# One transfer of 1 MB in place of two of 512 KB for each unit of weights

## What is computed

```python
for layer in range(2):
    h = h + hybrid_mixer(rms_norm(h, norm_mix_g[layer]), ...)   # w_in 1024x2560, w_out 1024x1024
    hn = rms_norm(h, norm_ffn_g[layer])
    if layer == 0: h = h + swiglu(hn, ffn_w1, ffn_w3, ffn_w2)      # 1024x3072, 1024x3072, 3072x1024
    else:          h = h + moe_swiglu(hn, router_w, expert_w1, expert_w3, expert_w2)
return rms_norm(h, final_g)                                     # 8 experts, top 2, hidden width 3584

def swiglu(x, w1, w3, w2):
    return (silu(x @ w1) * (x @ w3)) @ w2
```

## Time and profile before

| | us |
|---|---|
| median of 3 runs | 2086.88 |
| the profiled execution | 2092.64 |
| its span, first to last instruction | 2090.7 |
| TensorE matmuls busy | 2011.1 |
| VectorE busy | 1544.3 |
| ScalarE busy | 1207.3 |

### The profile page before, as it was taken

How to read it: one execution, slowest core, us unless ns; L and a number is a source line. 1 busy time by engine, 2 the same in 40 slices (tenths; PEclk the granted TensorE clock), 3 DMA queues, 4 the chain that set the end, 5 groups by cost and what they waited for, 6 DMA issues and landing times.

```text
span 2090.7 us, 33644 instructions
## 1 busy us (share of the span) xinstructions
PE 2011.1 (96%) x11091; PEld 1743.4 (83%) x11092; DVE 1544.3 (74%) x1694; ACT 1207.3 (58%) x1557; POOL 89.8 (4%) x132
## 2 busy tenths in 40 slices
PE   8999999999999998999999999999999999999992
PEld 7777888888897778999999888888998888888991
DVE  6896666666678976766766698898666888987655
ACT  4533555545554434554655577787555777875543
POOL 1000000000000003000000000000000000000002
PEclk9999999999999999999999999999999999999996
DMA  7321666666543214777777699999776999997743
GB/s 217 122 71 54 222 217 209 216 192 190 184 150 126 87 61 139 269 231 236 252 247 244 225 377 365 368 387 344 251 244 214 365 368 367 387 350 262 247 147 135
DMA packets 245442, 488.18 MB, mean 233 GB/s; under 512 B 16724, under 2 KB 86468, under 8 KB 245396
## 3 DMA queue, kind: packets, MB, share of 16 engines
q1 hardware_dynamic: 237668, 462.04, 64.8%
q0 software_dynamic: 7728, 25.52, 3.5%
HBM read 473.20 MB, written 14.30 MB: 233 GB/s over the span
## 4 chain that ended last, share of the span: by engine, by line
PE 78%; DVE 10%; issue 5%; ACT 3%; DMA 3%; POOL 1%; DVEq 0%; POOLq 0%; ACTq 0%; SPq 0%
PE PS L1430 76%; DVE wlo L724 2%; ACT whi L355 2%; DVE PS L865 2%; DMA raw<-in_expert_w 1%; DVE OV L839 1%; DVE OV L853 1%; DVE OV L1000 1%; PE PS L1758 1%; PE PS L1460 0%; DVE OV L869 0%; DMA OV<-in_norm_mix_g 0%; DVE OV L835 0%; DMA OV<-y_rows,addr 0%; PE PS L1682 0%
## 5 line engine op out<-in xcount | busy, mean ns | idle before, releaser
L724 DVE TENSOR_TENSOR wlo<-raw,whi 128x1024 fp32r<-128x1024 f32 x882 | 1044.0, 1221 | 154.8 <-ACT whi L355 149.1
L355 ACT ACTIVATE whi<-raw 128x1024 fp32r<-128x1024 f32 x882 | 896.7, 1053 | 156.1 <-DMA raw<-in_expert_w 76.6
L1430 PE MATMUL PS<-XN,whi 128*128 128x512 f32 (+3 forms) x3328 | 956.0, 363 | 15.0 <-DVE OV L1000 9.3
L1430 PE MATMUL PS<-XN,wlo 128*128 128x152 f32 (+3 forms) x2944 | 775.1, 263 | 0.0
L1430 PEld LDWEIGHTS PS<-XN,whi 128*128 128x128 f32 x3328 | 617.9, 189 | 84.1 <-DVE OV L1000 15.2
L1430 PE MATMUL PS<-whi,XN 128*128 128x512 f32 x2272 | 671.3, 394 | 8.8 <-DVE XN L874 3.5
L1430 PEld LDWEIGHTS PS<-XN,wlo 128*128 128x128 f32 x2944 | 561.1, 191 | 13.0
L1430 PEld LDWEIGHTS PS<-whi,XN 128*128 128x128 f32 x2272 | 423.6, 188 | 103.7 <-issue 6.9
L1430 PE MATMUL PS<-wlo,XN 128*128 128x512 f32 x1248 | 424.5, 391 | 0.0
L1430 PEld LDWEIGHTS PS<-wlo,XN 128*128 128x128 f32 x1248 | 234.4, 188 | 50.6
L567 ACT ACTIVATE OV<-PS 128x352 f32<-128x352 f32 x112 | 51.6, 461 | 139.9 <-PE PS L1430 139.9
(11 more groups left out here) (214 smaller groups left out, 967.0 us busy)
## 6 DMA issues: line engine op xcount, KB each, us to landing
raw<-in_expert_w SPq DMA_DIRECT2D x672, 512.0 KB, 5.1
raw<-in_ffn_w SPq DMA_DIRECT2D x144, 512.0 KB, 3.7
raw<-in_w_in SPq DMA_DIRECT2D x40, 512.0 KB, 5.4
raw<-in_w_out SPq DMA_DIRECT2D x16, 512.0 KB, 4.6
y_rows<-OV POOLq DMA_DIRECT2D x14, 512.0 KB, 4.4
y_rows<-OV POOLq DMA_DIRECT2D x14, 192.0 KB, 4.9
RES<-in_x SPq DMA_DIRECT2D x4, 512.0 KB, 5.8
x_tok<-OV POOLq DMA_DIRECT2D x4, 512.0 KB, 2.9
```

The source lines that it names most:

```text
L355: act.activation(whi[:, u0 % CONV, half(h)], raw[:, r, half(h)], ACT.Copy).then_inc(s["hi_done"], 1)
L724: dve.tensor_tensor(wlo[:, w, half(h)], raw[:, u0 % RAW, half(h)], whi[:, w, half(h)].bitcast(F32), ALU.subtract).then_inc(s["lo_done"], 1)
L1430: return pe.matmul(out_, lhsT, rhs, start=start, stop=stop, skip_group_check=True)
```

## The change

Each unit is brought by one transfer of 1 MB, which waits until both halves of the slot are done, and signals once. The six semaphores of `raw` become three. The splits stay in halves; the wait of both halves is now for the same semaphore.

```diff
@@ names
-... x3 raw00 raw01 raw10 raw11 raw20 raw21 prm_in ...
+... x3 raw0 raw1 raw2 prm_in ...
@@ load (SyncE)
-                for h in range(2):
-                    if not (isinstance(du, int) and u0 + du < RAW):
-                        sp.wait_ge(s["lo_done"], du * 2 + (2 * (u0 - RAW) + h + 1))
-                    sp.dma_start(raw[:, u0 % RAW, half(h)].rearrange("p (a b) -> p a b", a=parts // 2),
-                                 src[:, h * parts // 2:(h + 1) * parts // 2, :]).then_inc(s[f"raw{u0 % RAW}{h}"], 16)
+                if not (isinstance(du, int) and u0 + du < RAW):
+                    sp.wait_ge(s["lo_done"], du * 2 + (2 * (u0 - RAW) + 2))
+                sp.dma_start(raw[:, u0 % RAW, :].rearrange("p (a b) -> p a b", a=parts),
+                             src).then_inc(s[f"raw{u0 % RAW}"], 16)
@@ the 5 empty units at the end (SyncE)
-                for h in range(2):
-                    sp.wait_ge(s["lo_done"], n_more * (2 * UNITS) + (2 * (u - RAW) + h + 1))
-                    sp.sem_inc(s[f"raw{u % RAW}{h}"], 16)
+                sp.wait_ge(s["lo_done"], n_more * (2 * UNITS) + (2 * (u - RAW) + 2))
+                sp.sem_inc(s[f"raw{u % RAW}"], 16)
@@ split (ScalarE)
                 for h in halves:
-                    act.wait_ge(s[f"raw{r}{h}"], q * 16 + 16 * (u0 // RAW + 1))
+                    act.wait_ge(s[f"raw{r}"], q * 16 + 16 * (u0 // RAW + 1))
                     act.activation(whi[:, u0 % CONV, half(h)], raw[:, r, half(h)],
                                    ACT.Copy).then_inc(s["hi_done"], 1)
```

More of the change, by code:

```diff
@@ L154, in build_program @@
         l_rows = nc.dram_tensor("l_rows", [WIN * VIS, 1], U32)
-        names = """near_sel near_pos last_wout last_add last_ss last_xt last_T last_hi last_lo small_ok x0 x1 x2 x3 raw00 raw01 raw10 raw11 raw20 raw21 prm_in bd_in gB0_in gB_in gF_in rw_in
+        names = """near_sel near_pos last_wout last_add last_ss last_xt last_T last_hi last_lo small_ok x0 x1 x2 x3 raw0 raw1 raw2 prm_in bd_in gB0_in gB_in gF_in rw_in
           const_ok bd_zero step prm_T prm_ok lam_exp sp_ok rw_hi rw_ok warm_up
```

## The result

The changed kernel takes 2129.82 us (median of 4 runs, 2125.66 to 2132.54) and the kernel before 2088.03 (4 runs, 2086.76 to 2090.77). The ratio is 1.0195, with a 95% interval of 1.0175 to 1.0215. So the change costs 2.0%, some 42 us, where +6.8 us was predicted; the time lies above the stated range, which ended at 2117. The profiled execution took 2127.4 us, its span is 2125.7. (The profiled execution after the change is near the low end of its four runs; the one of before, 2092.64, lies above all four of its runs. So the two spans differ by less than the medians.)

The account below looks back on a forecast made before the run. TensorE was taken to bound the kernel, with transfers just keeping up in light visits. Terms 3.0 + 0.8 + 1.9 + 1.1 = +6.8 us took the profiled 2092.64 to 2099.4; predicted median 2093.7, range 2086 to 2117.

Parts of the forecast that it names:

- The landing: Time from issue of a 1 MB weight transfer until it has arrived in its slot, taken as 4.95 us.
- The hold: A ring slot is held from issue to the end of VectorE's second half: 0.1 + 4.95 + 3.45 = 8.50 us.
- That dense and heavy stages hide it: There three units' time exceeds the time a slot is held, by 7.7 us (dense) and 4.3 us (heavy): no loss.
- Light: 17.02 / 2 = 8.51, cover 0.01: In light expert groups, three units' time of 8.51 us just covers the 8.50 us a slot is held.
- lead of some 3.5 us that each of the two pairs of visits can spend first: Light visits: if the cover is gone, the splits' lead over TensorE absorbs some 3.5 us per pair before time is lost.
- Ring and lead, first of each pair handed over, second used up: Second light visit of each pair: lead falls from 3.0 us to -0.2; 1.5 us per pair, 3.0 in all.
- Ends of light visits: TensorE waits for `hidden_lo`, which stands behind a split that comes 0.2 us later: 0.2 x 4 = 0.8 us.
- Light to heavy: At two changes to heavy visits, two `whi` instead of one follow the chain's transfer: 0.95 x 2 = 1.9 us.
- Mixers: First mixer: first `whi` waits for its whole unit, +0.4; a later chain transfer brings +0.7; together 1.1 us.
- B: Ring becomes the bound if 1 MB takes 5.5 us: light groups 18.1 us, +28 us, 2115; chance 0.20.
- A: Cover holds in light groups if 1 MB lands in 4.7 us or less: +3 to +3.8 us, 2090 to 2091; chance 0.26.
- C: Faster: the chain's expert and mixer transfers land 2 us earlier: about -4 us, 2083; chance 0.08.

## Why the prediction was wrong

**Right, by its own steps.** 436 transfers of 1024 KB. The landing: 4.95 assumed, 5.0 measured. The conversion: 3.45 against 3.48 from landing to the end of the second `wlo`. The hold: 8.50 against 8.5 to 8.6 from issue to the end of the second `wlo` (means of the later groups of the visits 3 and 6), and 8.72 by half a group. That dense and heavy stages hide it: the merged transfers outside the experts cost 0.1%, and the heavy visits together took only 2.4 us more. That ScalarE's waits would be fewer and longer: 33 times, 34.6 us in 1314 to 1444, against 47 times and 20.1.

**The step that failed** is "Light: 17.02 / 2 = 8.51, cover 0.01", with what it allows after it: that a light group "neither loses nor gains lead", and the "lead of some 3.5 us that each of the two pairs of visits can spend first". It fails twice.

First, the hold was set against a steady group, and the ring's time has to be set against the whole visit. Around each change of visits the ring loses 7 to 9 us, standing still or waiting for late landings. The 0.8 us a group that the old ring gained, which the text did name, were not only for the gathers; they paid for all of this. Losing them leaves a deficit in every light visit. The three-quarter transfer shows it: with a round of 8.18, well on the safe side of 8.51, it still loses 0.8%.

Second, the lead could be spent only in part. In the place where the earlier trace rows gave a lead of 5.4 us, the group now starts at 1684.75, so that the same half is needed at 1693.0, and VectorE's two halves of that unit are these:

```profile
1689.31 2.36 DVE L722 TENSOR_TENSOR wlo<-raw,whi 128x1024 fp32r<-128x1024 f32 x2
```

The first ends at 1690.5, a lead of 2.5, while the groups are still 17.0 long: some 3 us were spent without a loss there. I took it that TensorE would go on until the lead over the splits was used up, and then wait for `wlo`. No matmul of line 1428 waits for `wlo` in a light visit. VectorE works in order, and `gated` stands behind the split of the unit that is used next, so TensorE already stops when the lead is down to 2.5 us; at the visit's end it stops at some 6, as `hidden_lo` stands behind the split of the seventh unit. (The last unit of visit 3 has a lead of 5.7 us before, 3.9 with 768 KB and 3.0 after, and the end is 0, 1.7 and 3.2 us longer than in the kernel before.) I had this second order in the text, and charged it only with the 0.2 us by which one landing would be later.

**The terms.** *Ring and lead, first of each pair handed over, second used up*: 3.0 predicted. Within the light visits, groups and all but the ends lost some 15.7 (28.9 for the four visits, less the ends). *Ends of light visits*: 0.8 predicted, 4 x 3.3 = 13.2 measured; moving the split shows that this is the same loss, collected at the end. *Light to heavy*: 1.9 predicted; the visits 4 and 7 lost 3.1 and 1.2, 4.3 together, which visit 0 (-2.3 us; its cause was not followed) partly hides. The landing there was 9.85 at 1470.09, as assumed against the 9.61 of the earlier trace rows. *Mixers*: 1.1 predicted, 2.9 in the profiled execution. These rows of the changed kernel's chain stand where the earlier trace rows has the transfer at 45.35 and the eviction at 52.92, now 2.93 later:

```profile
47.40 5.02 DMA raw<-in_w_in
...
52.53 2.01 ACT whi L353 x2
...
55.85 1.03 ACT OV L478
```

Two splits stand ahead of the eviction instead of one, as the prediction had it, but the transfer is also issued 2.05 later, so the units before it are late already. Most of that belongs to this one execution. Nine of the other kernels have the same transfers and splits in the mixers; the same eviction stands at 53.3 to 54.2 us in eight of them, 0.4 to 1.3 later than before, and at 55.4 in the ninth. In the kernel with the merged transfer outside the experts only, for one:

```profile
54.13 1.03 ACT OV L487
```

So the 1.1 was about right, and some 2 of the 35.0 us are no effect of the change. The first gather of the experts took about 1 us more.

**The rivals.** B had the mechanism, the ring as the bound, and was the nearest with +28. Its threshold was wrong: it was to decide from a landing of 4.96 on, and at 4.5 (the 768 KB) the loss has begun; its deduction of 7 us of lead was for a lead of which only a part can be spent. By its own test (groups over 17.3) it is the case that came. The sign that was given for A, that no matmul waits for `wlo`, came too, so it doesn't tell A from B. A fell by its landing, 5.0 where it wanted 4.7 or less, and by its price too: 4.5 doesn't cost +3 but 0.84%. C fell too: the chain's transfers end later, and the light visits move fewer bytes a second.

The Trainium skill's page "DMA: Bandwidth & Descriptors" asks, in its rules for kernel authors, for 1 MiB or more a transfer for full bandwidth. The measurement goes the other way in this kernel: 375 GB/s with halves and 347 with whole units in a light visit, which I put down to fewer bytes on their way in the three slots (argued, not shown by a run of its own). Its fit in "Anatomy of one DMA" (2.0 us + bytes / 436 GB/s), which gave case A its 4.4 us for 1 MB, is stated for transfers that GpSimd issues; the prediction left that out. The weights are issued by SyncE, and here the median was 5.0.

## What to carry to other kernels

Work out the cover of a ring of buffers over the whole period, with the stretches in which it stands still, and not over one steady group: slots times period, less the standstill, over the number of fillings, against issue, landing and conversion. A lead is worth only what the consumer can reach of it; look for the first instruction of an in-order engine that stands behind a late one and is itself waited for. Halving what a slot waits for was worth more here, with three slots, than larger transfers: giving it up at the issue alone cost 1.6%, at the signal alone 2.4%. A wait that can be moved by reordering isn't yet a wait that is gone.

## What the runs showed of the hardware

- Two transfers of 512 KB issued 0.5 us apart finish later (5.9 to 7.0 us in the chain for the second) than one of 1 MB in the same ring (4.76 and 5.14 in the chain above).
- The engines' busy share doesn't show the lost throughput: 389 GB/s at a share of 1.03 before, 360 GB/s at 1.00 after.
- 768 KB took 4.5 us in the median, 1 MB 5.0. The quarter saved 0.5 where the rate of 389 GB/s would give 0.7.
- With 30 matmuls added at the ends of light visits, TensorE stood still for 8.69 and 8.31 us at 1021 and 1670 us, of which 5.40 at 1015.86 are time in which nothing that the profile shows was waited for; heavy visit 1 took 195.5 us there for 184.4, and visit 5 143.2. With 16 matmuls it didn't occur. The cause stays open.
